# Value banks, third projection's bank, meta loads and rotary turns of a hybrid decoder layer

## The reference

```
q  = rmsnorm(c_q) @ w_q_up            # 8 heads x (128 plain + 64 rotary)
kv = rmsnorm(c_kv) @ w_kv_up          # 8 heads x (128 keys + 128 values)
q_rope = rope(q_rope); k_rope = rope(k_rope)     # [x1 cos - x2 sin, x2 cos + x1 sin]
att = softmax(causal(q k^T * scale)) @ v
y_meta, st = ssd_chunked(xs[:, :16], dt, a, bm, cm, 0, 16)       # state after the meta positions
y_real, _  = ssd_chunked(xs[:, 16:], dt, a, bm, cm, st, 128)
```

## Time and profile before

| | |
|---|---|
| median of 3 runs | 1700.35 us (1698.83 to 1702.49) |
| profiled execution | 1699.8 us, span 1698.0 us |
| mean granted clock of TensorE | 0.976 |
| TensorE matmul / weight load busy | 1596.5 us (94%) / 1366.9 us (81%) |
| VectorE, ScalarE, GpSimd busy | 946.7, 607.8, 807.5 us (56%, 36%, 48%) |
| rotary q | from 359.6 to 395.5 us |
| attention block | 395.5 to 725.5 us |
| last head of it | from about 680 us |

### The profile page before, as it was taken

The page is one execution under the profiler, slowest core; times in us unless marked ns, Lnnn a source line. Parts: engine busy times, 40 slices in busy tenths (PEclk is TensorE's granted clock), DMA queues, the critical chain, the costliest instruction groups (busy, mean ns, idle before and its releaser), DMA issues.

```text
span 1698.0 us, 23372 instructions
## 1 busy us (share of the span) xinstructions
PE 1596.5 (94%) x8143; PEld 1366.9 (81%) x8143; DVE 946.7 (56%) x1551; ACT 607.8 (36%) x1181; POOL 807.5 (48%) x765
## 2 busy tenths in 40 slices
PE   3999999987999999889999999999999999999995
PEld 3999998866888888668888778888888888888884
DVE  5555515155667666547778765874444444444446
ACT  5322312233444444345555343232223233333333
POOL 7152544144565663724322324375555555555553
PEclk8999999998999999789999999999999999999998
DMA  6343522226355543478887652011111111111116
GB/s 201 77 133 110 176 63 63 65 68 172 119 171 150 153 119 106 157 262 292 293 293 263 249 189 75 13 50 50 49 57 65 58 49 49 49 49 49 50 56 100
DMA packets 181863, 204.24 MB, mean 120 GB/s; under 512 B 18336, under 2 KB 145152, under 8 KB 181792
## 3 DMA queue, kind: packets, MB, share of 16 engines
q1 hardware_dynamic: 180496, 199.12, 36.8%
q0 software_dynamic: 1296, 4.19, 1.5%
HBM read 133.97 MB, written 69.30 MB: 120 GB/s over the span
## 4 chain that ended last, share of the span: by engine, by line
PE 64%; DVE 5%; ACT 2%; DMA 2%; issue 1%; POOL 1%; SPq 0%; POOLq 0%; DVEq 0%
PE ps L2550 17%; PE ps L2536 16%; PE ps L2400 5%; PE ps L1541 4%; PE ps L2516 3%; PE ps L2502 3%; PE ps L1466 2%; PE ps L1514 2%; PE ps L1486 2%; PE ps L1527 1%; PE ps L2356 1%; PE ps L1511 1%; PE ps L2585 1%; PE ps L1512 1%; PE ps L2380 1%
## 5 line engine op out<-in xcount | busy, mean ns | idle before, releaser
L3012 DVE TENSOR_TENSOR acc<-ps,acc 128x512 f32<-128x512 f32 x208 | 142.3, 690 | 114.9 <-PE ps L2550 114.9
L163 POOL TENSOR_TENSOR ring<-stage,zero 128x512 fp32r<-128x512 f32 (+2 forms) x79 | 88.2, 1117 | 205.2 <-PE ps L716 62.4
L2550 PE MATMUL ps<-wdhi,fshi 128*128 128x512 f32 x416 | 161.8, 389 | 0.0
L2550 PE MATMUL ps<-wdhi,fslo 128*128 128x512 f32 x416 | 161.8, 389 | 0.0
L2550 PE MATMUL ps<-wdlo,fshi 128*128 128x512 f32 x416 | 161.8, 389 | 0.0
L2274 POOL TENSOR_TENSOR wdlo<-wd_b,wdhi 128x512 fp32r<-128x512 f32 x56 | 70.7, 1293 | 140.6 <-ACT wdhi L2786 140.6
L3040 DVE TENSOR_TENSOR ps<-ps,fs_b 128x512 f32<-128x512 f32 x42 | 29.3, 699 | 150.7 <-PE ps L2536 150.7
L165 POOL TENSOR_TENSOR ring<-stage,ring 128x512 fp32r<-128x512 f32 (+2 forms) x79 | 104.2, 1318 | 6.2
L716 PE MATMUL ps<-hThi,ring 128*128 128x346 f32 x512 | 99.5, 325 | 0.3 <-PEq L252 0.3
L2550 PEld LDWEIGHTS ps<-wdhi,fshi 128*128 128x128 f32 x416 | 78.1, 188 | 16.3 <-issue 0.2
L2550 PEld LDWEIGHTS ps<-wdhi,fslo 128*128 128x128 f32 x416 | 78.1, 188 | 16.3
(11 more groups left out here) (478 smaller groups left out, 4727.9 us busy)
## 6 DMA issues: line engine op xcount, KB each, us to landing
wd_b<-w_mlp_down SPq DMA_DIRECT2D x28, 512.0 KB, 4.0
wA_b<-w_mlp_up SPq DMA_DIRECT2D x42, 256.0 KB, 2.8
stage<-w_in SPq DMA_DIRECT2D x40, 256.0 KB, 2.7
stage<-w_out SPq DMA_DIRECT2D x32, 256.0 KB, 3.8
xt<-x SPq DMA_DIRECT2D x8, 512.0 KB, 7.5
d_xT<-xdT SPq DMA_DIRECT2D x8, 512.0 KB, 3.3
d_x<-x_tok SPq DMA_DIRECT2D x8, 512.0 KB, 4.6
d_zT<-zs SPq DMA_DIRECT2D x16, 256.0 KB, 2.3
```

Source lines behind the costliest of these rows:

```text
L163: pool.tensor_tensor(hi, src, k.zero[:, 0:1].broadcast_to([P, width]), ALU.add).then_inc(k.sem(fam + "_hi"), 1)
L2550: mm = pe.matmul(ps[:, 2 + n % 4, :], fs[a][:, j, P * t:P * t + P], half(wd[b][:, j, :], c), start=(j == 0 and a == 0 and b == 0), stop=(j ...
L3012: dve.tensor_tensor(part, ps[:, 2 + n % 4, :], part, ALU.add).then_inc(sem("v_added"), 1)
```

## The change

Five things. In rotary q, `turn_qr` and `low_qr` come two tiles behind the matmuls and rotations instead of one; TensorE starts after 6 latents; VectorE's half reads q from PSUM instead of `zs`, so tile t waits for VectorE's two products of tile t-4 (`qro_step0`). In attention, value pieces use OUT and PROJ by turns, and the waits follow: piece n waits for piece n-2, and the next head's first q piece for value piece 3. Projection piece 2 goes to OUT: it waits for the first output half, piece 3 for piece 1, and the last turned batch for piece 2. In the last head, SyncE issues the meta loads before head 6's second output store instead of behind it. And the meta x is scaled, and its low part made, by GpSimd (between `sel` and `run`) instead of VectorE; ScalarE makes the high part in block 4 instead of 3.

```diff
@@ -568,7 +568,7 @@
         if t == 0:
             eng.wait_ge(sem("rope_in"), 16)
             eng.wait_ge(sem("kro_done"), 2)
-        q = zs[:, t % 4, :].rearrange("p (h c) -> p h c", c=ROPE)
+        q = (zs[:, t % 4, :] if half else ps[:, t % 4, :]).rearrange("p (h c) -> p h c", c=ROPE)
         x = (q[:, :, 0:32], q[:, :, 32:64])
         cos = rope[:, t, 0:32].unsqueeze(1).broadcast_to([P, HEADS, 32])
         sin = rope[:, t, 32:64].unsqueeze(1).broadcast_to([P, HEADS, 32])
@@ -820,12 +820,13 @@
                     mm = pe.transpose(ps[:, 4 + t % 2, P * i:P * i + P], qro[:, t % 2, 2 * i:2 * i + 2, :].rearrange("p a b -> p (a b)"), k.ident[:, :])
                 mm.then_inc(sem("qr_turned"), 1)
 
-            pe.wait_ge(sem("lat_lo"), 13)
+            pe.wait_ge(sem("lat_lo"), 6)
             for t in range(NT):
                 if t < 4:
                     pe.wait_ge(sem("zs_done"), 2 * NT)
                 else:
                     pe.wait_ge(sem("qr_raw"), t - 3)
+                    pe.wait_ge(sem("qro_step0"), 2 * (t - 3))
                 for kk in range(KQ):
                     if t == 0:
                         pe.wait_ge(sem("w_cut"), nb + kk + 1)
@@ -833,9 +834,10 @@
                         mm = pe.matmul(ps[:, t % 4, :], k.cqT[a][:, kk, P * t:P * t + P], W[b][:, (nb + kk) % RING, :],
                                        start=(kk == 0 and (a, b) == (0, 0)), stop=(kk == KQ - 1 and a == 1))
                 mm.then_inc(sem("qr_done"), 1)
-                if t:
-                    turn_qr(t - 1)
-            turn_qr(NT - 1)
+                if t >= 2:
+                    turn_qr(t - 2)
+            for t in (NT - 2, NT - 1):
+                turn_qr(t)
 
         @block.scalar
         def _(act):
@@ -1140,9 +1142,10 @@
 
             for t in range(NT):
                 rotate_half(dve, t, 0, ta, tb)
-                if t:
-                    low_qr(t - 1)
-            low_qr(NT - 1)
+                if t >= 2:
+                    low_qr(t - 2)
+            for t in (NT - 2, NT - 1):
+                low_qr(t)
             dve.wait_ge(sem("p_exp"), 1)
             dve.tensor_tensor(k.dend[:, :, :], k.dend[:, :, :], k.dt[:, :, :], ALU.mult).then_inc(sem("p_dtd"), 1)
 
@@ -1275,10 +1278,13 @@
     PIECE = (("q", 0), ("k", 0), ("k", 1), ("q", 1), ("k", 2))
     NEED = {0: 2, 2: 3, 4: 4, 5: 5}
 
+    def piece_bank(n):
+        return OUT if n == 2 else PROJ
+
     def turn_bank(b, i):
         return OUT if b == NT - 1 and i == NB - 1 else TURN + i % 2
 
-    def evacs(n, u, bank=PROJ):
+    def evacs(n, u, bank):
         pbank = ps[:, bank, :]
         kind, c = PIECE[n]
         if kind == "q":
@@ -1286,11 +1292,14 @@
         c0, w = TC[c]
         return [(ps[:, bank, 0:w], [x[:, c0:c0 + w] for x in kT[u]])]
 
+    def v_bank(n):
+        return (OUT, PROJ)[n % 2]
+
     def evac_v(n):
 
         if n == VPIECES - 1:
-            return ps[0:META, OUT, 0:2 * VH].rearrange("p (u c) -> p u c", u=2), [x[0:META, :, NT, :] for x in v]
-        return ps[:, OUT, :].rearrange("p (t u c) -> p t u c", t=2, u=2), [x[:, :, 2 * n:2 * n + 2, :].rearrange("p u t c -> p t u c") for x in v]
+            return ps[0:META, v_bank(n), 0:2 * VH].rearrange("p (u c) -> p u c", u=2), [x[0:META, :, NT, :] for x in v]
+        return ps[:, v_bank(n), :].rearrange("p (t u c) -> p t u c", t=2, u=2), [x[:, :, 2 * n:2 * n + 2, :].rearrange("p u t c -> p t u c") for x in v]
 
     PIECES = 5
     NE = PIECES
@@ -1331,6 +1340,15 @@
             def pieces(h, first, last):
                 for p in list(range(AT[h], AT[h + 1]))[first:last]:
                     store_piece(p)
+
+            def meta_loads():
+                for sent in ("xp_sent", "xp_wsent"):
+                    sp.wait_ge(sem(sent), 32 * NP)
+                sp.wait_ge(sem("a_proj"), PIECES * HEADS)
+                sp.wait_ge(sem("a_vproj"), VPIECES * HEADS // 2)
+                sp.dma_start(k.zs[0:META, :], k.d_xm).then_inc(sem("s_start_in"), 16)
+                for i in range(2):
+                    sp.dma_start(k.bt[i][0:META, :].bitcast(F32), k.d_bm[i]).then_inc(sem("s_start_in"), 16)
 
             def head(h, u, left, pairs=None):
 
@@ -1347,6 +1365,8 @@
                 pieces(h, 2, 3)
                 outputs(h, 0)
                 pieces(h, 3, None)
+                if left == 1:
+                    meta_loads()
                 outputs(h, 1)
 
             for q in range(2):
@@ -1359,13 +1379,6 @@
                 head(h, h % 2, 2, h // 2 if h % 2 == 0 else None)
             head(HEADS - 2, 0, 1)
 
-            for sent in ("xp_sent", "xp_wsent"):
-                sp.wait_ge(sem(sent), 32 * NP)
-            sp.wait_ge(sem("a_proj"), PIECES * HEADS)
-            sp.wait_ge(sem("a_vproj"), VPIECES * HEADS // 2)
-            sp.dma_start(k.zs[0:META, :], k.d_xm).then_inc(sem("s_start_in"), 16)
-            for i in range(2):
-                sp.dma_start(k.bt[i][0:META, :].bitcast(F32), k.d_bm[i]).then_inc(sem("s_start_in"), 16)
             for n in range(STAGES):
                 load_block(sp, k, "u", n, k.wo_blocks[n])
             for i in range(2):
@@ -1438,6 +1451,11 @@
             for e in range(2):
                 pool.tensor_tensor(k.sel[:, :, e, 64 * e:64 * e + 64], k.pick[:, :].bitcast(F32).unsqueeze(2).broadcast_to([P, 4, 64]),
                                    k.zero[:, 0:4].unsqueeze(2).broadcast_to([P, 4, 64]), ALU.add).then_inc(sem("s_sel"), 1)
+            xm, xwm = k.zs[0:META, :], k.es[0:META, :, :].rearrange("p a b -> p (a b)")
+            pool.wait_ge(sem("s_start_in"), 16 * 3)
+            pool.tensor_tensor(by_heads(xwm), by_heads(xm), per_head(k.dend[0:META, NT, :], META), ALU.mult).then_inc(sem("p_xw"), 1)
+            pool.wait_ge(sem("p_xwhi"), 1)
+            pool.tensor_tensor(k.xh0[1][0:META, :], xwm, k.xh0[0][0:META, :].bitcast(F32), ALU.subtract).then_inc(sem("p_xwlo"), 1)
             pool.wait_ge(sem("s_run_lo"), 1)
             for q in range(SH // 4):
                 pool.tensor_tensor(k.run[0][:, 4 * q:4 * q + 4, :], k.turned[:, 0, :].bitcast(F32).unsqueeze(1).broadcast_to([P, 4, P]),
@@ -1455,10 +1473,12 @@
 
                 if n < 2:
                     pe.wait_ge(sem("a_cut"), 4 * h + 2 + 2 * n)
-                bank = FIRST_BANKS[n] if first else PROJ
+                bank = FIRST_BANKS[n] if first else piece_bank(n)
                 pbank = ps[:, bank, :]
-                if not first:
-                    pe.wait_ge(sem("a_e_lo"), NE * h + n)
+                if not first and n == 2:
+                    pe.wait_ge(sem("a_o_lo"), 2 * h)
+                elif not first:
+                    pe.wait_ge(sem("a_e_lo"), NE * h + (2 if n == 3 else n))
                 kind, c = PIECE[n]
                 if kind == "q":
                     for kk in range(KQ):
@@ -1478,12 +1498,14 @@
                 if n == 0:
                     pe.wait_ge(sem("a_v_cut"), 2 * i + 2)
                     pe.wait_ge(sem("a_o_lo"), 4 * i + 1)
+                elif n == 1:
+                    pe.wait_ge(sem("a_e_lo"), 2 * NE * i + NE)
                 else:
-                    pe.wait_ge(sem("a_v_lo"), VPIECES * i + n)
+                    pe.wait_ge(sem("a_v_lo"), VPIECES * i + n - 1)
                 for j, c0 in [(0, 0)] if n == VPIECES - 1 else [(j, META + P * (2 * n + j)) for j in range(2)]:
                     for kk in range(KK):
                         for a, b in PASSES:
-                            mm = pe.matmul(ps[:, OUT, 2 * VH * j:2 * VH * j + 2 * VH], k.ckT[a][:, kk, c0:c0 + P], wv[b][:, kk, :, :].rearrange("p u c -> p (u c)"),
+                            mm = pe.matmul(ps[:, v_bank(n), 2 * VH * j:2 * VH * j + 2 * VH], k.ckT[a][:, kk, c0:c0 + P], wv[b][:, kk, :, :].rearrange("p u c -> p (u c)"),
                                            start=(kk == 0 and (a, b) == (0, 0)), stop=(kk == KK - 1 and a == 1))
                 mm.then_inc(sem("a_vproj"), 1)
 
@@ -1514,12 +1536,14 @@
                         mm = pe.matmul(out, qr[u][a][:, q], k.krT[:, c0:c1], start=False, stop=(a == 1))
                 mm.then_inc(sem("a_s"), 1)
 
-            def turn(h, b):
+            def turn(h, b, more=True):
 
                 pe.wait_ge(sem("a_p"), NT * h + b + 1)
                 for i, (_, p0, np_) in of_block(b):
                     if turn_bank(b, i) == OUT:
                         pe.wait_ge(sem("a_o_lo"), 2 * h + 2)
+                        if more:
+                            pe.wait_ge(sem("a_e_lo"), NE * h + NE + 3)
                     elif i >= 2:
                         pe.wait_ge(sem("a_t_lo"), NB * h + i - 1)
                     for j in range(np_):
@@ -1571,6 +1595,8 @@
                     for n in V_AT.get(b, ())[:1] if u == 0 else ():
                         values(i, n)
                     if more and b in (5, 6):
+                        if b == 5 and u == 0:
+                            pe.wait_ge(sem("a_v_lo"), VPIECES * i + 4)
```

(16 more changed lines are left out.)

## The result

The changed kernel takes **1673.39 us** (median of 4 runs, 1673.14 to 1673.66). The kernel before took 1699.59 us beside it (4 runs, 1697.01 to 1702.49). The ratio is 0.9845 with a 95% interval of 0.9828 to 0.9862: 26.2 us less.

A forecast was written before the change was run, and what follows sets the result against it. TensorE's waits were taken to bound the kernel; gains of 9.2 + 8.2 + 2.0 - 0.4 = 19.0 us took the median from 1700.35 to 1681.3 us. Whole range 1676 to 1688, the forecast's own 1679 to 1684.

The forecast's parts named there:

- Rotary q, 9.2 us: Rotary q stage: earlier start and quicker tiles make attention begin sooner, 9.2 us gained, bounds 7 and 10.
- Values, 8.2: Attention's value pieces: two alternating banks remove TensorE's 8 stops, 8.2 us gained, bounds 6 and 8.2.
- third piece, 2.0: Third projection piece in the output bank: no wait for the piece before's cut, 2.0 us gained, bounds 1.5 and 2.0.
- the third rival: Attention heads: value stops come back further on, half of 8.2 and all of 2.0 lost, 1687.4 us; chance 0.15.
- I take the full 8.2: Value pieces: the whole listed idle of TensorE's stops, 8.2 us, counted as gain.
- Meta positions, +0.4: Last head: TensorE's stop shrinks, but GpSimd's added work closes the block 0.4 us later; bounds 4.5 earlier, 2.5 later.
- The rival that this work hides: Last head: GpSimd's two meta operations fit before its input arrives, 4.5 us sooner, 1676.5 us; chance 0.12.
- The rest, 0 forecast: Stages behind the attention block: no change, 0 us.
- Half clock at the start of rotary q: Rotary q's start: TensorE at half clock costs 1.65 us; with slower tiles 1685.0 us, joint chance 0.14.
- The slower pace of 2.7 us a tile: Rotary q: contended GpSimd costs another 2 us; with half clock at the start 1685.0 us, joint chance 0.14.
- the slower side: Last head: clock stays down behind the new 3.6 us stop, 14 us slower, 1714 us; chance 0.02.

The follow-up runs named there:

- The single runs: The kernel before with only the two value banks (1690.29 us), and with only projection piece 2 in the output bank (1697.54 us).
- rot_sbuf: The changed kernel, but VectorE too reads q from ScalarE's copy in SBUF: 1678.45 us, ratio 0.9882.
- meta_only: The kernel before with only the sooner meta loads and their product and low part on GpSimd: 1697.40 us, ratio 0.9981.

## Why the prediction was off

*Rotary q, 9.2 us: right in size and in its steps.* First tile forecast at 359.8, found 359.88; last store landing and last copy 381.6, found 381.64; attention 386.3, found 386.32. GpSimd's period was forecast at 2.45 and is 2.5. The experiments split it as said: the earlier start counts because ScalarE's copy of tile 0 and the rotations follow it, not for TensorE's own sake. One thing the forecast kept apart belongs together: where VectorE reads q from decides GpSimd's pace too (2.51 or 2.70 us a tile).

*Values, 8.2, and third piece, 2.0: the right waits, the wrong price.* All fifteen stops went, the added waits cost nothing, and neither came back further on (the third rival falls). The failed step is "I take the full 8.2", with its upper bound 8.2: I read the listed idle as all that a stop costs. Start to start it is 1.33 or 1.23 us for a value stop (1.08 or 0.97 listed) and 0.60 for a third-piece stop (0.34 listed), by the rows 10.2 and 3.9 us in all. The single runs gave 9.8 to 10.7 and 2.9 to 3.8, the changed kernel 13.8 for both. The two terms together (10.2) were 3.6 us short and made the largest part of the miss. Since the listed figure was also the upper bound, the range could not take it in.

*Meta positions, +0.4: the mechanism was right, the size 1.2 us off.* The product took 2.02 (forecast 1.9), the low part 2.33 (2.4), TensorE stood 3.19 (3.6), and GpSimd's drain ended 5.9 us after TensorE's, so it closes the block as forecast. `run` started 0.5 us later after `one` than before (15.44 against 14.9) where 0.9 was forecast; its four products took 4.28 in all where they had taken 5.21, 0.9 less (the product of 2.02 in the earlier trace rows is gone), of which the forecast had counted half; and the twelve cuts and the drain behind them took 0.4 us less than before. 0.5 - 0.9 - 0.4 is the -0.8 of the table. The rival that this work hides falls: it would have needed `run` at 10.4 behind `one`. The rule of the Trainium skill that I had weighed ("GPSIMD Engine Reference", section 4.1, twice VectorE's time) gave an estimate of 2.4 and 3.4; measured are 2.02 and 2.33 beside VectorE's 1.21 and 1.69, 1.7 and 1.4 times. Of these, VectorE's 1.21 was taken with GpSimd idle, its 1.69 beside GpSimd's first `run` product (from 689.27), so the 1.4 does not compare the two engines each alone.

*The rest, 0 forecast, 2.9 found: nothing ties it to the change.* The code behind attention is the same in all twelve kernels, and their profiles have 966.5 to 973.4 us there, mean 969.7; the kernel before (one profile) was the second slowest of them and the kernel after at the mean. One place is the MLP's first matmul. The table by stretches, the kernel before and then after, each for the 5.8 us behind that stop:

```profile
1019.20:1025.00 5.80, 5.80 (x14) 4.54 (x15) 5.13 (x11) 1.35 (x3) 0.00 (x0) 0.50 0.00 0
```

```profile
993.90:999.70 5.80, 5.79 (x18) 4.60 (x19) 5.13 (x11) 1.35 (x3) 0.00 (x0) 0.71 0.00 0
```

The stop was 3.40 us before and is 2.21 after, and behind it 14 matmuls fit in where after 18 do. Why this stop and its clock vary from profile to profile the runs don't tell, and it does not set the stage's length by itself: `meta_only` has the stop at 3.33 us and one of the shortest stages, 968.30. The forecast gave this stage no width, which was an error of its own: a profiled execution is a draw from a spread of 7 us there. Had I taken 13.7 for the heads and +0.4 for the last head, the forecast would have been 1700.35 - 22.5 = 1677.8, inside the range but still 4.4 us over the result; of these, 1.2 are the last head, 0.8 that the kernel before itself came out at 1699.59 beside the result, and the 2.4 that are left lie within this spread.

*The other rivals.* Half clock at the start of rotary q did not come: 1.00 in both stretches. The slower pace of 2.7 us a tile came only in `rot_sbuf`, where it cost 3.1 us in all and not the 2 of the rival. The clock in the last head came back within 4 us, so the slower side never stood near.
